# The second layer's value projection moved ahead as seven half-size products, and its head steps cut to three weight chunks

## The chip, the cores and the metric

The kernel runs on one core of a Trainium2 chip. The metric is the device time in microseconds from the first to the last instruction of one execution, taken as the median of several runs. In the profile the engines are PE (TensorE matmul), PEld (its weight loads), DVE (VectorE), ACT (ScalarE), POOL (GpSimd) and SP (SyncE, which here only issues DMAs).

## The reference, cut to what matters

Two transformer blocks run one after the other over 512 tokens with 2048 channels, in float32. The first block is untouched except that work is put beside its last two stages. The second block is

```
h = x1 @ w_in_2                       # 2048 -> 8192 columns
qa, ka, va, ga, qb, kb, vb, gb = split(h)      # 1024 columns each, 16 heads of 64
ya = dilated_attention(qa, ka, va) * silu(ga)        # 16 heads "A"
yb = neighbourhood_attention(qb, kb, vb) * silu(gb)  # 16 heads "B"
out = layer_norm(alpha * x1 + concat(ya, yb) @ w_out_2)
```

`x1` is the first block's output. The change concerns `va` and `vb` (all 2048 value columns) and the order of the work around the two attentions.

## The kernel before, in words

Every float32 matrix product is done as three matmuls on split operands: high part by high part, low by high and high by low (`mm3`, L454 to L458). Weights come as one stream of chunks of 1 MB (128 partitions x 2048 float32). SP loads a chunk into one of two buffers `w_raw`, ACT copies its high part into `w_hi` (`split_hi`, L436 to L440), DVE subtracts to get `w_lo` (`split_lo`, L442 to L445), and PE uses both (`chunk_ready`). The counters `hi_ready`, `lo_ready` and `chunk_used` count chunks; chunk c can be split once chunk c-2 has been used. A chunk of 256 weight columns and 8 tiles of the inner dimension takes 48 matmuls of 512 columns.

The stages that matter, in order of time:

- **Up** (about 1157 to 1325 us): 8 groups of two chunks (`up_group` on PE, `up_out` on DVE). For each group POOL loads 1.5 MB of gates (`load_gates`, L2905) into the single tile `mixg` once DVE has read the last ones; DVE's first use (`gated`, L2406) stands ahead of its `split_lo` of the next group's first chunk.
- **Output projection of block 1** (about 1326 to 1500 us): 8 groups of two chunks (`wo_group` on PE, `x1_out_of` on DVE). It leaves x1 in `act_b`, high and low parts, two of 16 tiles per group. DVE adds the residual (L2445), ACT makes the high part, DVE the low part (L2452).
- **Head-pair steps** (about 1500 to 2286 us): 16 groups of four chunks. Step s multiplies x1 with the columns of query, key, value and gate of one pair of heads (128 columns each): chunks cc 0 and 1 give query and key, cc 2 and 3 give value and gate. In the same step PE does the attention of the pair before it, in two bursts (`beat`): ahead of chunk 0, and ahead of chunk 2. A burst has the logits of two units (`qk2`, L1160) and the products of two earlier units' probabilities with the values (`pv2`, L1181). Steps 1 to 8 attend over A heads (kind "A2"), steps 9 to 16 over B heads ("M2" on PE, "N2" on POOL).
- **Last product** (2286 us to the end): `w_out_2`, then the layer norm.

Between logits and `pv2` a unit goes through a chain: DVE adds the bias and takes the maximum (`soft2_a`, L2472 or L2476), ACT takes the exponential (`exp2`), DVE divides by the sum (`soft2_b`, L2492 and L1806) and transposes 32x32 blocks (`flip2`, L2505 or L2510), POOL stores the result to HBM (`flip_store`, L2989) and loads it back turned (`flip_load`, L3000, into `prob_t`). For A heads units 0 and 1, whose logits are in the first burst, are read by the second burst of the same step, and units 2 and 3 by the first burst of the next step. For B heads every unit is read one whole step later. The values are transposed by DVE (L2589), stored (L2970) and loaded as `v_tok_a` or `v_tok_n` (L2977, L2980) in every step. At each step's end ACT takes a tanh of the gate (L1749) and DVE finishes it (L2593).

All orders are written out by hand, one in-order program per engine, with semaphores between them.

Of the kernel before, what the change touches and what calls it, by code (L numbers as in the profile page):

```python
# [19 lines left out]
F32 = mybir.dt.float32  # L20
# [5 lines left out]
P = 128  # L26
# [20 lines left out]
G_UP, G_WO, G_IN2, G_OUT2 = 52, 60, 68, 100  # L47
N_GROUPS = 108
G_S0, G_S1 = G_Q + 2, G_MIX + 6
C_S0 = 2 * G_S0  # L50
SLOT_KB = (16, 20, 32, 36, 24, 28, 40)

# [83 lines left out]
def build_kernel(nc, wst, xt_in, mem_in, par_in, con_in, pos_in, tab1_in, tab2_in, rpb_in, lng_in, lnb_in, out):  # L136
# [18 lines left out]
    v2_d = nc.dram_tensor("v2_d", [T, P], F32)  # L155
# [6 lines left out]
    with ctx:  # L162
# [86 lines left out]
        th_2 = sb_at("th_2", [P, 2, T], RA + 44 * KB)  # L249

# [98 lines left out]
        par_s, con_s, pos_s = sem("params_loaded"), sem("con_loaded"), sem("pos_loaded")  # L349
# [4 lines left out]
        mem_s = [sem(f"mem_loaded{i}") for i in range(8)]  # L354
        x_s = [sem(f"x_loaded{i}") for i in range(8)]
        mh_s, ml_s = sem("mem_hi"), sem("mem_lo_and_x_sums")
        sq_s, sq_used, rows_s = sem("squares_and_x_sums_hi"), sem("squares_used_and_x_sums_lo"), sem("row_sums_copied_and_quarter_chain")
        stm_s, stx_s = sem("mem_sums_psum"), sem("x_sums_psum")
# [43 lines left out]
        v2_stored, v2_loaded = sem("v2_stored"), sem("v2_loaded")  # L402
# [33 lines left out]
        def split_hi(act, c, s, early=False):  # L436

            act.wait_ge(w_loaded[s], 8 * (c - s) - 16)
            act.wait_ge(chunk_used, c - 3 if early else c - 1)
            act.activation(w_hi[s][:], w_raw[s][:], ACT.Copy).then_inc(hi_ready, 1)  # L440

# [105 lines left out]
        def in2_banks(kind, cc):  # L547

            return (0, 1) if cc < 2 or kind == "A2" else (4, 5) if kind else (6, 7)
# [34 lines left out]
        def _(sp):  # L584
# [46 lines left out]
            with sp.Fori(G_IQ, G_OUT2 + 1) as g:  # L631
                for s in range(2):
                    sp.wait_ge(lo_ready, 2 * g + s - 1)
                    sp.dma_start(w_raw[s][:], wst[2 * g + s]).then_inc(w_loaded[s], 16)

            def last_weights(c):
                sp.wait_ge(lo_ready, c - 1)
                sp.dma_start(w_raw[c % 2][:], wst[c]).then_inc(w_loaded[c % 2], 16)
# [5 lines left out]
            sp.wait_ge(chunk_used, 2 * G_OUT2 - 1)  # L644
# [29 lines left out]
        def _(pe):  # L674
# [512 lines left out]
            pe.wait_ge(x1f_s, 18)  # L1187
            pe.wait_ge(x1h_s, 9)
            pe.wait_ge(x1l_s, 7)
# [20 lines left out]
            def pair_step(step, par, kind, before, gemm=True):  # L1210

                for cc in range(4):
                    if kind and cc % 2 == 0:
                        beat(kind, before, step, cc // 2, par)
                    g = 2 * step + (G_IN2 + cc // 2)
                    if cc % 2 == 0 and before:
                        if kind == "A2" or (before == "A2" and cc == 0):
                            pe.wait_ge(ev_act, evac_act(step, cc // 2 - 1))
                            pe.wait_ge(ev_dve, evac_dve(step, cc // 2 - 1))
                        elif before == "M2":  # L1220
                            pe.wait_ge(ev_act, evac_act(step - 1, cc // 2))
                            pe.wait_ge(ev_dve, evac_dve(step - 1, cc // 2))
                    elif cc == 2 and kind:
                        pe.wait_ge(ev_act, evac_act(step, 0))
                        pe.wait_ge(ev_dve, evac_dve(step, 0))
                    chunk_ready(pe, 2 * g + cc % 2)
                    rows_t(pe, cc % 2, range(6), act_b, in2_banks(kind, cc))
                    if cc == 1 and not kind:
                        pe.wait_ge(x1h_s, 10)
                        pe.wait_ge(x1l_s, 8)  # L1230
                    rows_t(pe, cc % 2, range(6, 8), act_b, in2_banks(kind, cc)).then_inc(chunk_used, 1)
# [8 lines left out]
            with pe.Fori(0, 3) as i:  # L1240
                pair_step(2 * i + 10, 1, "M2", "M2")
                pair_step(2 * i + 11, 0, "M2", "M2")
            def y_split(pe, k):
# [34 lines left out]
            pe.wait_ge(ev_act, evac_act(15, 1))  # L1278
            pe.wait_ge(ev_dve, evac_dve(15, 1))
# [47 lines left out]
        def _(act):  # L1327
# [368 lines left out]
            with act.Fori(0, 4) as i:  # L1696
                for s in range(2):
                    g = 2 * i + (G_WO + s)
                    hi2(g)
                    act.wait_ge(x1f_s, 4 * i + (2 * s + 6))  # L1700
                    copy(act_b[0][:, bass.ds(4 * i + 2 * s, 2), :], stage[s][:]).then_inc(x1h_s, 1)
# [21 lines left out]

            def pair_step(step, par, kind, before, new, final=False):

                for cc in range(4):
                    g = 2 * step + (G_IN2 + cc // 2)
                    if kind:
                        split_hi(act, 2 * g + (cc % 2 + 1), 1 - cc % 2)
                        if cc % 2 == 0:  # L1730
                            for c in (cc, cc + 1):
                                exp2(kind, step, c)
                    if new:
                        if not kind:
                            split_hi(act, 2 * g + (cc % 2 + 1), 1 - cc % 2)
                        if cc == 1:
                            summed(g)
                            dst, src = q_rows(new, qkvg[1 - par][0][:], bank[0][:])
                            copy(dst, src)
                            dst, src = q_rows(new, q_raw[new == "N2"][:], bank[0][:])  # L1740
                            copy(dst, src).then_inc(ev_act, 1)
                        elif cc == 3:
                            if final:
                                for p in range(2):
                                    y_hi(p)
                            summed(g)
                            if not (isinstance(step, int) and step == 0):
                                act.wait_ge(ev_dve, evac_dve(step - 1, 1))
                            act.activation(th_2[:, par, :], bank[in2_banks(kind, cc)[1]][:], ACT.Tanh, scale=0.5).then_inc(ev_act, 1)  # L1749
# [13 lines left out]
            split_hi(act, 2 * G_OUT2 + 1, 1)  # L1763
# [5 lines left out]
            split_hi(act, 2 * G_OUT2 + 2, 0)  # L1769
            split_hi(act, 2 * G_OUT2 + 3, 1)  # L1770
# [3 lines left out]
            def last_split_hi(c):  # L1774

                act.wait_ge(w_loaded[c % 2], 8 * (2 * G_OUT2 + c - c % 2) - 16)
# [3 lines left out]
            def rows_out(n_out):  # L1780
                for c in range(1 if n_out else 3, 5):
# [3 lines left out]
                    if 4 * n_out + c < 13 and (n_out or c > 3):  # L1785
                        split_hi(act, 2 * G_OUT2 + 4 * n_out + c, c % 2)
# [13 lines left out]
        def _(dve):  # L1800
# [636 lines left out]
            def x1_out_of(i, s):  # L2437
# [8 lines left out]
                if not (isinstance(i, int) and i == 3):  # L2446
# [4 lines left out]
                dve.wait_ge(x1h_s, 2 * i + (s + 3))  # L2451
                dve.tensor_tensor(act_b[1][:, bass.ds(4 * i + 2 * s, 2), :], stage[s][:],  # L2452
                                  act_b[0][:, bass.ds(4 * i + 2 * s, 2), :].bitcast(F32), ALU.subtract).then_inc(x1l_s, 1)

# [81 lines left out]
            def beat_dve(kind, before, step, cc, par, split):  # L2536

                if cc % 2 == 0:
                    if cc == 0 and kind == "A2":
                        dve.wait_ge(b2_loaded[par], bias2_count(step, par))  # L2540
                    elif cc == 0:
                        dve.wait_ge(nb_ready, 2 * step - 16)
                    for c in (cc, cc + 1):
                        soft2_a(kind, step, c, par)
                    split()
                    for c in (cc, cc + 1):
                        soft2_b(kind, step, c)
                        if kind == "A2" or c % 2:
                            flip2(kind, step, c)
                else:  # L2550
                    if before == ("A2" if cc == 1 else "M2"):
                        gated2(before, step - 1, 1 - par)
                    split()

            def pair_step(step, par, kind, before, new, final=False):

                for cc in range(4):
                    g = 2 * step + (G_IN2 + cc // 2)
                    split = lambda: split_lo(dve, 2 * g + (cc % 2 + 1), 1 - cc % 2)
                    if kind:  # L2560
                        beat_dve(kind, before, step, cc, par, split)
                    if new:
                        if not kind:
                            split()
                        if cc == 1:
                            summed(g)
                            q_l, k_l = qk_lo(new, 1 - par)
                            q_h, k_h = qkvg[1 - par][0:2]
                            if new == "A2" and isinstance(step, int) and step == 0:
                                for s in range(2):  # L2570
                                    dve.wait_ge(x1_out[s], 416)
                            dve.tensor_scalar(k_h[:], bank[1][:], HD2 ** -0.5, None, ALU.mult).then_inc(x1h_s, 1)
# [558 lines left out]
```

## Time and profile before

| | us |
|---|---|
| median of 3 runs | 2478.37 (2478.15 to 2479.02) |
| span of the profiled execution | 2477.0 |
| PE busy in the profiled execution | 2464.3 (99%) |
| DVE, ACT, POOL busy | 1506.1, 841.0, 696.6 |
| mean granted TensorE clock | 0.999 |
| DMA, mean over the span | 183 GB/s |

A busy time counts an engine's instructions, not its waits. PE's busy time is near the span because its matmuls follow each other; each is listed with some 390 ns though one starts every 227 ns, since they overlap in the array. So distances between start times are read, not durations. The profiled execution's own time is known only as this span, which lies 1.4 us under the median of the runs.

### The profile page before, as it was taken

What the parts mean: (1) busy time and instruction counts of PE and PEld (TensorE: products, weight loads), DVE (VectorE), ACT (ScalarE), POOL (GpSimd) and SP (SyncE); (2) the same over time, 40 slices, a digit from 0 to 9 for tenths busy, and PEclk for the clock granted to TensorE, in tenths of its full rate; (3) what the DMA queues carried; (4) which work ended last, traced back from release to release, by engine and by line L of the source; (5) the groups of instructions that cost most, each with busy time, mean ns of one, the idle gap of its engine ahead of it and who ended that gap; (6) DMA issues with size and microseconds to landing.
All of it is one profiled execution on the core that took longest, in us unless ns stands there. A gap on an engine that the chain in (4) does not pass through costs nothing.

```text
span 2477.0 us, 36169 instructions
## 1 busy us (share of the span) xinstructions
PE 2464.3 (99%) x13712; PEld 2092.3 (84%) x13712; DVE 1506.1 (61%) x2529; ACT 841.0 (34%) x1281; POOL 696.6 (28%) x867
## 2 busy tenths in 40 slices
PE   9999999999999999999999999999999999999998
PEld 7788899999988888888888888888888888888887
DVE  5664877898779976655554333556465545455525
ACT  7422444544454333333222222223232322223221
POOL 0312455666512222232001220211122334343100
PEclk9999999999999999999999999999999999999999
DMA  7748333433456766777544444676656555546622
GB/s 287 223 162 271 114 126 128 130 135 136 137 173 211 259 230 237 241 244 274 178 165 149 136 153 128 205 196 205 205 176 212 172 175 160 171 153 214 242 96 102
DMA packets 102405, 452.53 MB, mean 183 GB/s; under 512 B 18006, under 2 KB 18006, under 8 KB 74182
## 3 DMA queue, kind: packets, MB, share of 16 engines
q1 hardware_dynamic: 38712, 241.58, 28.7%
q0 software_dynamic: 63568, 209.25, 26.8%
q8 instruction: 82, 1.34, 0.2%
q14 instruction: 43, 0.35, 0.0%
HBM read 351.47 MB, written 100.79 MB: 183 GB/s over the span
## 4 chain that ended last, share of the span: by engine, by line
PE 98%; DMA 1%; SPq 0%; DVE 0%; ACT 0%; issue 0%; DVEq 0%
PE bank L456 23%; PE bank L457 22%; PE bank L458 22%; PE bank L874 16%; PE bank L1258 5%; PE bank L1181 2%; PE bank L1319 2%; PE bank L1160 2%; PE bank L1043 1%; PE bank L1018 1%; DMA w_raw<-wst 1%; PE bank L955 1%; PE bank L1038 0%; PE bank L1008 0%; PE bank L898 0%; PE bank L713 0%
## 5 line engine op out<-in xcount | busy, mean ns | idle before, releaser
L445 DVE TENSOR_TENSOR w_lo<-w_raw,w_hi 128x2048 fp32r<-128x2048 f32 x164 | 375.9, 2292 | 369.5 <-ACT w_hi L440 367.3
L456 PE MATMUL bank<-act_b,w_hi 128*128 128x512 f32 x1280 | 501.6, 392 | 0.0
L457 PE MATMUL bank<-act_b,w_lo 128*128 128x512 f32 x1280 | 498.4, 389 | 0.0
L458 PE MATMUL bank<-act_b,w_hi 128*128 128x512 f32 x1280 | 498.1, 389 | 0.0
L440 ACT ACTIVATE w_hi<-w_raw 128x2048 fp32r<-128x2048 f32 x163 | 311.7, 1913 | 509.6 <-PE bank L458 435.9
L456 PE MATMUL bank<-act_a,w_hi 128*128 128x512 f32 (+1 forms) x1032 | 405.8, 393 | 0.0
L457 PE MATMUL bank<-act_a,w_lo 128*128 128x512 f32 (+1 forms) x1032 | 401.9, 389 | 0.0
L458 PE MATMUL bank<-act_a,w_hi 128*128 128x512 f32 (+1 forms) x1032 | 401.8, 389 | 0.0
L456 PEld LDWEIGHTS bank<-act_b,w_hi 128*128 128x128 f32 x1280 | 240.2, 188 | 54.5 <-issue 5.2
L458 PEld LDWEIGHTS bank<-act_b,w_hi 128*128 128x128 f32 x1280 | 240.3, 188 | 50.4
L457 PEld LDWEIGHTS bank<-act_b,w_lo 128*128 128x128 f32 x1280 | 240.3, 188 | 48.8
L874 PE MATMUL bank<-t_xh,pt_w 128*128 128x256 f32 x1280 | 232.1, 283 | 0.0
L456 PEld LDWEIGHTS bank<-act_a,w_hi 128*128 128x128 f32 (+1 forms) x1032 | 193.4, 187 | 42.3 <-issue 1.4
L458 PEld LDWEIGHTS bank<-act_a,w_hi 128*128 128x128 f32 (+1 forms) x1032 | 193.4, 187 | 41.2
L457 PEld LDWEIGHTS bank<-act_a,w_lo 128*128 128x128 f32 (+1 forms) x1032 | 193.5, 188 | 39.1
L874 PEld LDWEIGHTS bank<-t_xh,pt_w 128*128 128x128 f32 x1280 | 199.7, 192 | 0.0
L874 PE MATMUL bank<-act_a,pt_w 128*128 128x256 f32 x1440 | 181.5, 283 | 0.0
L874 PE MATMUL bank<-t_xl,pt_w 128*128 128x256 f32 x640 | 181.1, 283 | 0.0
L2105 DVE TENSOR_TENSOR pt_w<-s_sum,pt_w 128x512 fp32r<-128x512 f32 x160 | 157.9, 1003 | 37.1 <-ACT pt_w L1332 36.3
L874 PEld LDWEIGHTS bank<-act_a,pt_w 128*128 128x128 f32 x1440 | 176.2, 192 | 3.0 <-issue 1.6
L2766 POOL TENSOR_TENSOR s_sum<-w_raw 128x512 f32<-128x512 f32 x80 | 120.7, 1520 | 108.7 <-DMA w_raw<-wst 70.4
L1332 ACT ACTIVATE pt_w<-s_sum 128x512 fp32r<-128x512 f32 x160 | 100.5, 630 | 94.0 <-PE bank L874 82.9
(376 smaller groups left out, 3351.7 us busy)
## 6 DMA issues: line engine op xcount, KB each, us to landing
w_raw<-wst SPq DMA_DIRECT2D x210, 1024.0 KB, 5.0
prob_t<-flip_d POOLq DMA_DIRECT2D x64, 512.0 KB, 4.8
flip_d<-flip POOLq DMA_DIRECT2D x56, 512.0 KB, 4.3
mix_d<-stage POOLq DMA_DIRECT2D x24, 512.0 KB, 3.2
mixg<-mix_d POOLq DMA_DIRECT2D x8, 1536.0 KB, 6.8
prob_tk<-flip_d POOLq DMA_DIRECT2D x32, 256.0 KB, 6.0
flip_d<-flip_a POOLq DMA_DIRECT2D x16, 512.0 KB, 2.9
b<-rows_2d POOLq DMA_DIRECT2D x16, 448.0 KB, 10.3
```

The lines of the kernel that those rows point to most:

```text
L440: act.activation(w_hi[s][:], w_raw[s][:], ACT.Copy).then_inc(hi_ready, 1)
L445: dve.tensor_tensor(w_lo[s][:], w_raw[s][:], w_hi[s][:].bitcast(F32), ALU.subtract).then_inc(lo_ready, 1)
L456: pe.matmul(out_ap, l_hi, r_hi, start=start, stop=False)
L457: pe.matmul(out_ap, l_lo, r_hi, start=False, stop=False)
L458: return pe.matmul(out_ap, l_hi, r_lo, start=False, stop=stop)
L874: last = pe.matmul(quarter(g, i), pt_w[i][l][:, j, :], x_part(c, i, r, j), start=(i % 2 == 0 and c == 0 and j == 0 and m == 0), stop=(c == ...
L1160: ins = pe.matmul(logit_bank(kind, step, cc, e)[:, off:off + w], q[half, c * P:(c + 1) * P], keys(k, half), start=(n == 0), stop=(n == 2))
L1181: last = pe.matmul(bank[O_BANK][64 * e:64 * e + 64, c * P:(c + 1) * P], v[:, b, 64 * e:64 * e + 64], turned[:, e, b], start=(b == 0), stop ...
L1258: last = pe.matmul(bank[4 * s + b][:], act_b[l][:, k, b * P:(b + 1) * P], wt(r[c % 2], kt, 0, 2 * GC, 2 * GC), start=(k == 0 and n == 0), ...
L1332: return act.activation(dst, src, ACT.Copy, **kw)
L2105: dve.tensor_tensor(pt_w[i][1][:], w_part(c, i), pt_w[i][0][:].bitcast(F32), ALU.subtract)\
L2766: pool.tensor_tensor(dst[:], l, r, op).then_inc(ws_s, 1)
```

## The change

Value columns leave the head-pair steps. Before step 0 a new stage computes all values at once. For each of the two layers' halves (n = 0: A heads, n = 1: B heads) the 512 x 2048 by 2048 x 1024 product is cut in halves in all three dimensions and done as seven products of 256 tokens x 1024 x 512 columns (the Winograd form of Strassen's scheme), each of two chunks of 24 matmuls. The tokens are now the stationary operand.

- Weight sums: four per half, each 2 MB, made HBM to HBM by POOL's DMAs during the up stage (`w_sums_2`: four copies, then four accumulating DMAs in three stages, each after the one before).
- Sums of x1: DVE makes four of 128x256 per tile pair in the output projection, POOL stores them and loads them back at the stage's start, ACT and DVE split them.
- Results: ACT and DVE combine the seven products from PSUM (`values_first`, `values_read`), POOL stores 16 tiles to HBM (`values_store`).
- Three raw weight buffers instead of two in this stage.

A step then has three chunks: two for query and key, one for the gate (PSUM bank 7). The second burst stands in the middle of the second chunk for A heads (k = 12 of 16), and between the second and the third chunk for B heads. DVE's transpose of the values and POOL's store of them go; `load_v` loads from the table.

DVE's order in a step of kind "A2" changes too, see below. The load of the attention outputs for the last product (`load_y`) waits for the middle of step 15's gate chunk; it waited for the chunk ahead of the last one.

```diff
@@ SP
+            for n in range(2, PARTS_V):
...
+                sp.dma_start(w_raw_v[slot][:], src).then_inc(wv_loaded[slot], 16)
...
-            sp.wait_ge(chunk_used, 2 * G_OUT2 - 1)
+            sp.wait_ge(half_g, 17)
@@ PE: the new stage
+                for kc in range(2):
+                    c = C_VAL + 2 * p + kc
+                    chunk_ready(pe, c)
+                    for jj in range(4):
+                        j = 4 * kc + jj
...
+                        for b in range(2):
+                            for m, (l, r) in enumerate(((0, w_hi), (1, w_hi), (0, w_lo))):
+                                last = pe.matmul(v_banks(p)[b][:], v_stationary(q, l, j, b), wt(r[c % 2], jj, 0, 512, 512),
+                                                 start=(j == 0 and m == 0), stop=(j == 7 and m == 2))
+                    last.then_inc(chunk_used, 1)
@@ PE: a step
+                if kind:
+                    beat(kind, before, step, 0, par)
...
+                for m in range(2):
...
+                        if kind == "A2" and k == A2_BEAT:
+                            beat(kind, before, step, 1, par)
...
+                if kind == "M2":
+                    beat(kind, before, step, 1, par)
...
+                for k in range(KT):
+                    last = mm3(pe, bank[G_BANK][:], ...)
+                    if last_step and k == CK - 1:
+                        last.then_inc(half_g, 1)
@@ DVE: output projection
+                dve.tensor_tensor(t1, b12, b11, ALU.subtract).then_inc(xs_new_s, 1)
+                dve.tensor_tensor(t3, b22, b12, ALU.subtract).then_inc(xs_new_s, 1)
...
+                dve.tensor_tensor(t2, b22, t1, ALU.subtract).then_inc(xs_new_s, 1)
...
+                dve.tensor_tensor(t4, t2, b21, ALU.subtract).then_inc(xs_new_s, 1)
@@ DVE: a step of kind "A2", m = 1
+                        if m == 1 and before == "A2":
+                            gated2(before, step - 1, 1 - par)
+                        split()
+                        if m == 1:
+                            for c in (2, 3):
+                                soft2_a(kind, step, c, par)
...
+                    if new and m == 1:
+                        dve.wait_ge(chunk_used, in2_chunk(step, 2))
...
+                        dve.tensor_scalar(k_h[:], bank[1][:], HD2 ** -0.5, None, ALU.mult).then_inc(x1h_s, 1)
...
+                        dve.tensor_tensor(q_l[:], q_raw[new == "N2"][:], q_h[:].bitcast(F32), ALU.subtract)\
+                            .then_inc(x1l_s, 1)
+                    if kind == "A2" and m == 1:
+                        for c in (2, 3):
+                            soft2_b(kind, step, c)
                             flip2(kind, step, c)
@@ POOL: up stage
+            def w_sums_2(v, stage_):
+                if v or stage_:
+                    pool.wait_ge(ws_done, 128 * v + (0, 64, 96, 112)[stage_])
+                if stage_ == 0:
+                    for dst, summand in ((2, 0), (0, 2), (1, 3), (3, 1)):
+                        w_sum(v, dst, "w", summand)
+                elif stage_ == 1:
+                    w_sum(v, 2, "w", 2, True)
+                    w_sum(v, 0, "w", 3, True)
...
+            for j in range(1, 8):
                 pool.wait_ge(up_ev, 3 * j + 3)
                 pool.nop(nofuse=True)
                 load_gates(j)
+                w_sums_2((j - 1) // 4, (j - 1) % 4)
```

## Rows read from the trace of the kernel before

**Rows 1.** The page: shares of the chain that ended last, by engine.
```profile
PE 98%; DMA 1%; SPq 0%; DVE 0%; ACT 0%; issue 0%; DVEq 0%
```

**Rows 2.** Waits of PE: who waited for whom, total us, times, longest.
```profile
PE bank L742 <- POOL warm L2682: 1.6, 1, 1.6
```

**Rows 3.** The chain in order of time: start us, length us, what.
```profile
1643.92 1.59 PE bank L1160 x12
1645.52 1.90 PE bank L1181 x32
...
1694.90 1.59 PE bank L1160 x12
...
2045.36 0.93 PE bank L1160 x12
2046.29 1.02 PE bank L1181 x16
...
2286.64 1.59 PE bank L1258 x6
...
2324.28 98.15 PE bank L1258 x432
```

**Rows 4.** Timeline of DVE, second burst of an A step: start, us, instruction, idle before.
```profile
1669.48 0.69 DVE L2572 TENSOR_SCALAR qkvg<-bank 128x512 fp32r<-128x512 f32 x1 [6.64 <-PE bank L458]
...
1676.65 0.16 DVE L2492 RECIPROCAL rden<-rs 128x1 f32<-128x1 f32 x1
```

**Rows 5.** Timeline of POOL in the same step, both bursts.
```profile
1660.88 0.77 POOL L3000 DMA_DIRECT2D prob_t<-flip_d  x1 [1.84 <-DMA flip_d<-flip_a]
...
1685.91 0.77 POOL L3000 DMA_DIRECT2D prob_t<-flip_d  x1 [0.57 <-DMA flip_d<-flip_a]
```

**Rows 6.** The tile prob_t, 30 loads of 1575 to 1945 us: issue to landing.
```profile
DMA to landing us min/median/max: 4.1/4.6/8.3
```

**Rows 7.** Timeline of DVE and ACT around the output projection's end.
```profile
1489.54 1.92 ACT L440 ACTIVATE w_hi<-w_raw 128x2048 fp32r<-128x2048 f32 x1 [6.60 <-PE bank L458]
...
1491.49 2.29 DVE L445 TENSOR_TENSOR w_lo<-w_raw,w_hi 128x2048 fp32r<-128x2048 f32 x1 [6.22 <-ACT w_hi L440]
1500.42 1.29 DVE L2445 TENSOR_TENSOR stage<-bank,xr 128x512 f32<-128x512 f32 x2 [6.64 <-PE bank L458]
1502.95 1.23 DVE L2452 TENSOR_TENSOR act_b<-stage,act_b 128x1024 fp32r<-128x1024 f32 x1 [1.23 <-ACT act_b L1332]
```

**Rows 8.** Timeline of SP, ACT and DVE at the last steps' end.
```profile
2273.84 1.02 SPq L642 DMA_DIRECT2D o_raw<-y_d  x2
...
2280.05 1.92 ACT L1332 ACTIVATE act_b<-o_raw 128x2048 fp32r<-128x2048 f32 x1 [4.23 <-DMA o_raw<-y_d]
...
2286.78 0.58 ACT L1749 ACTIVATE th<-bank 128x512 f32<-128x512 f32 x1
...
2292.01 2.28 DVE L2388 TENSOR_TENSOR act_b<-o_raw,act_b 128x2048 fp32r<-128x2048 f32 x1
```

**Rows 9.** Timeline of DVE and POOL in one group of the up stage.
```profile
1195.85 1.29 DVE L2406 SCALAR_TENSOR_TENSOR m_tmp<-mixg,bank 128x512 f32<-128x512 f32 x2 [4.25 <-PE bank L458]
...
1205.06 1.29 DVE L2406 SCALAR_TENSOR_TENSOR m_acc<-mixg,bank 128x512 f32<-128x512 f32 x2 [1.26 <-DMA mixg<-mix_d]
1208.61 2.29 DVE L445 TENSOR_TENSOR w_lo<-w_raw,w_hi 128x2048 fp32r<-128x2048 f32 x1 [2.26 <-ACT w_hi L440]
...
1197.98 0.77 POOL L2905 DMA_DIRECT2D mixg<-mix_d  x1 [20.80 <-DVE m_tmp L2406]
```

**Rows 10.** DMA of 210 to 250 us, GB/s in 40 slices of 1 us; one issue.
```profile
GB/s 315 381 340 250 410 397 397 414 270 205 131 115 102 111 102 94 102 111 164 193 295 344 393 410 430 397 418 463 422 389 430 414 401 348 348 352 262 94 16 0
...
rows_n<-rpb POOLq DMA_DIRECT2D x1, 1472.0 KB, 14.9
```

**Rows 11.** Timeline of POOL and DVE in a step over B heads.
```profile
2119.20 7.86 POOL L2959 TENSOR_TENSOR nb<-nl,con 128x256 f32<-128x256 f32 x8 [8.82 <-DMA nl<-rows_n]
...
2126.56 1.25 DVE L2510 STREAM_TRANSPOSE flip_n<-prob 128x1024 f32<-128x1024 f32 x1
```

More of the change, by code:

```diff
@@ L440, in split_hi, with split_hi2, raw_slot, raw_loads @@
             act.activation(w_hi[s][:], w_raw[s][:], ACT.Copy).then_inc(hi_ready, 1)
+        def split_hi2(act, c, s):
+            act.wait_ge(w_loaded[s], 8 * (c - s) - (16 + 8 * (PARTS_V - 2)))
+            act.wait_ge(chunk_used, c - 1)
+            act.activation(w_hi[s][:], w_raw[s][:], ACT.Copy).then_inc(hi_ready, 1)
+        def raw_slot(n):
+            return n if n < 2 else 0 if n == 2 else (2, 1, 0)[n % 3]
+        def raw_loads(n):
+            return sum(raw_slot(m) == raw_slot(n) for m in range(2, n + 1))
+        def v_banks(n):
+            return [bank[2 * (n % 4) + b] for b in range(2)]
+        def v_used(n):
+            return C_VAL + 2 * n + 2
+        def in2_chunk(step, m):
+            return 3 * step + (C_IN2 + m)
+        def in2_buf(par, m):
+            return (m + 1 - par) % 2
         def split_lo(dve, c, s):
@@ L630, in _ @@
                 weights(c)
-            with sp.Fori(G_IQ, G_OUT2 + 1) as g:
+            with sp.Fori(G_IQ, G_VAL + 1) as g:
                 for s in range(2):
@@ L1208, in beat @@
                         pv2("M2", step - 1, cc, 1 - par)
[L1210 to L1231, printed above, removed]
@@ L1722, in y_hi @@
                 copy(act_b[0][:, k0:k1, :], o_raw[:, k0:k1, :]).then_inc(oh_s, 1)
-            def pair_step(step, par, kind, before, new, final=False):
[L1726 to L1749, printed above, removed]
@@ new lines, in values_first @@
+            def values_first(n):
+                if n:
+                    act.wait_ge(v2_ready, 8 * n + 16)
+                else:
+                    act.wait_ge(x1f_s, 20)
+                act.wait_ge(chunk_used, v_used(7 * n))
+                for b in range(2):
+                    last = copy(v_sum[b][:], v_banks(7 * n)[b][:])
+                last.then_inc(v_first, 1)
+            for n in range(1, PARTS_V):
+                values_hi(n)
+                if n in (2, 4, 6, 8):
+                    x_sums_hi(n // 2 - 1)
+                if n % 14 == 3:
+                    values_first(n // 14)
@@ new lines, in _ @@
+            split_hi2(act, C_IN2, 0)
+            def pair_step(step, par, kind, before, new, final=False):
+                for m in range(3):
+                    if kind or new:
+                        split_hi2(act, in2_chunk(step, m + 1), in2_buf(par, m + 1))
+                    if kind and m == (0, 1 if kind == "A2" else 2)[m > 0]:
+                        for c in (0, 1) if m == 0 else (2, 3):
+                            exp2(kind, step, c)
+                    if new and m == 1:
+                        act.wait_ge(chunk_used, in2_chunk(step, 2))
+                        dst, src = q_rows(new, qkvg[1 - par][0][:], bank[0][:])
+                        copy(dst, src)
+                        dst, src = q_rows(new, q_raw[new == "N2"][:], bank[0][:])
+                        copy(dst, src).then_inc(ev_act, 1)
+                    elif new and m == 2:
+                        if final:
+                            for p in range(2):
+                                y_hi(p)
+                        act.wait_ge(chunk_used, in2_chunk(step, 3))
+                        if not (isinstance(step, int) and step == 0):
+                            act.wait_ge(ev_dve, evac_dve(step - 1, 1))
+                        act.activation(th_2[:, par, :], bank[G_BANK][:], ACT.Tanh, scale=0.5).then_inc(ev_act, 1)
@@ L2534, in last_lo @@
                     .then_inc(olo_s, 1)
[L2536 to L2548, printed above, removed]
-                            flip2(kind, step, c)
[L2550 to L2553, printed above, removed]
@@ new lines, in values_read @@
+            def values_read(n, q):
+                dve.wait_ge(chunk_used, v_used(7 * n + q))
+                if q == 1:
+                    dve.wait_ge(v_first, n + 2)
+                elif q > 2:
+                    dve.wait_ge(v_read, 3 * n + {3: 2, 4: 3, 5: 3, 6: 4}[q])
+                src = v_banks(7 * n + q)
+                for b in range(2):
+                    if q == 1:
+                        values_out(n, b, 0, src[b][:], v_sum[b][:], ALU.add)
+                    elif q == 2:
+                        last = dve.tensor_tensor(v_sum[b][:], src[b][:], v_sum[b][:], ALU.subtract)
+                    elif q == 3:
+                        last = dve.tensor_tensor(v_rest[b][:], v_sum[b][:], src[b][:], ALU.subtract)
+                    elif q == 4:
+                        values_out(n, b, 1, v_rest[b][:], src[b][:], ALU.subtract)
+                    elif q == 5:
+                        values_out(n, b, 2, src[b][:], v_rest[b][:], ALU.add)
+                        last = dve.tensor_tensor(v_sum[b][:], src[b][:], v_sum[b][:], ALU.add)
+                    else:
+                        values_out(n, b, 3, src[b][:], v_sum[b][:], ALU.subtract)
+                if q in V_SUMS:
+                    last.then_inc(v_read, 1)
```

344 lines of the change are left out of this document (262 added, 82 removed).

## The prediction

> **What bounds the kernel now.** I read the chain that ended last first. 98% of it is PE [rows 1], so a gain must come from fewer matmuls, and any new wait of PE is paid in full. The waits of PE came second: it waits for another engine once to a visible extent, 1.6 us at the start [rows 2]. Third, the chain in order of time, for distances. From one first burst to the next an A step takes 1694.90 - 1643.92 = 50.98 us, of which a burst is 1.59 + 1.90 = 3.49 us, twice; a burst over B heads is 0.93 + 1.02 = 1.95 us. In the last product 432 matmuls take 98.15 us, 0.2272 us each [rows 3]. An A step's 192 matmuls take (50.98 - 6.98) / 192 = 0.229 us each, the same plus a refill behind each burst. So I count 0.227 us per matmul of 512 columns, 10.9 us per chunk of 48. Last I read DVE, ACT and POOL around the two bursts, since that slack is what the change spends.
>
> **The saving.** The steps lose one chunk of 48 matmuls each, 16 x 48 = 768. The new stage has 2 x 7 products x 8 tiles x 2 token blocks x 3 = 672. Both have 512 moving columns, and with tokens stationary the last product runs at 0.2272 us [rows 3]. Net 96 x 0.227 = **-21.8 us**. All else is at best neutral.
>
> **The second burst of an A step.** In the new order DVE takes the maximum for units 2 and 3, then waits for the end of the second chunk, makes the key and query parts, and only then divides, transposes and hands units 2 and 3 to POOL. The next step's first burst needs them. Take the second chunk's end as 0.
> - DVE starts the key part 0.4 us after a chunk's end (the burst's first matmul at 1669.06 by the same timeline, the key part at 1669.48 [rows 4]) and has three instructions of 0.69 us that overlap slightly: divisions begin at 2.5.
> - From the first reciprocal to the issue of the last `prob_t` load is 1685.91 - 1676.65 = 9.26 us [rows 4, 5], and the load lands 4.6 us later in the median, 4.1 to 8.3 [rows 6]. DVE's split stands ahead of that chain before and behind it after, so it is not in these 9.26. The last unit is there at 2.5 + 9.3 + 4.6 = 16.4.
> - PE wants it after the gate chunk, 10.9, then the logits, 1.6, then the product with the other unit, 0.95 (half of 1.90): 13.5 with 0.1 for the switch.
> So PE waits 2.9 us. DVE's split of the next chunk now ends about when the two loads are issued (2.5 + 5.1 of divisions and transposes + 2.3 = 9.9), and frees a raw buffer: a 1 MB weight load starts beside them. At the 410 GB/s of full slices [rows 10] 1 MB is 2.6 us; I give the last load 0.6 us of it. That makes 3.5 us per step, in steps 2 to 9 (the first burst of each reads A units of the step before): 8 x 3.5 = **+28 us**. Bounds: 2.4 us with the shortest landing and no contention, 19 in all; 5 us if a load takes 6.5 us, 40 in all. Before, the same units had 1676.65 - 1669.06 = 7.6, + 9.3 + 4.6 = 21.5 us against 21.8 + 3.5 + 2.6 = 27.9, so 6 us of slack; one chunk less with the key part kept ahead of them uses more than that.
>
> Units 0 and 1 have less trouble. Their last load is issued 1660.88 - 1643.92 = 17.0 us after the burst's start [rows 3, 5] and lands at 21.6; PE wants it at 3.5 + 10.9 + 5.5 + 1.6 + 0.95 = 22.4, later still by the 3.5 us that PE has just waited. I cost it at nothing; without that cover it is 0 to 1 us.
>
> **Steps over B heads.** A step shrinks to 144 x 0.227 + 3.9 = 36.6 us. Units are read a step later, so the DMA round trip has room. DVE is the fuller engine: its transpose ends at 2126.56 + 1.25, 10.6 us behind the key part's start (2117.20 by the same view) [rows 11]; after it comes the 0.85 us of the output gate, all before the gate chunk ends (10.9 + 1.95 = 12.9). POOL's 7.86 us of window bias begins 9 to 10 us after its loads' issue and ends near 32 of 36.6 us. Nothing; if one of them is late, some 1 us x 8.
>
> **The new stage.** A chunk of 24 matmuls takes 5.45 us. Splitting one takes 1.92 on ACT and 2.29 on DVE; ACT starts at the earlier chunk's end and DVE ended at 1493.78, 4.2 us after ACT's start at 1489.54 [rows 7], some 4.6 after the chunk's end. It fits with 0.8 us left. Reading a product adds two PSUM operations of 0.65 (four after the sixth), 1.3 or 2.6 us of DVE per two chunks: 4.6 + 2.6 = 7.2, while the next split can begin at 5.45 + 2.3 = 7.8. Nothing in the likeliest case; 0.5 us in each of 27 chunks, 13 us, if waits between them add up.
> Its start is late. DVE begins the last x1 tiles at 1500.42 and ends their low part at 1504.18 [rows 7]. Then come the four new sums of 128x256 (about 0.4 each, under the 0.65 of 512 columns, with two hand-overs: 1.8) and the split of the second chunk, 2.3: 1508.3. PE ends the first chunk at 1500.1 + 5.45 = 1505.6: **+2.7 us**. Its end is smooth but for one weight load that must land in 6.2 us: +0.3.
>
> **The end.** The loads for the last product are issued 5.4 us ahead of step 15's end instead of 10.9. The first was split by ACT 6.2 us after issue [rows 8], so at +0.8, +2.7 done, +5.0 with DVE's 2.3. PE comes to it 2.0 us after the end (2286.64 - 2284.6 [rows 3]): some 3 us of wait. The second load delays ACT's tanh and all of DVE's later work by 3 to 6 us, and DVE's low part before ended at 2294.3, just ahead of PE [rows 8]; both shift together. **+3 us**, bounds 1 and 6.
>
> **The up stage.** POOL queues 8.4 MB of copies and later 4.2, 2.1 and 2.1 MB of accumulating DMAs behind one gate load and ahead of the next. Now DVE's first gate use starts 7.1 us after the issue and is followed by the split at 1208.61, which PE needs at 1195.4 + 21.8 = 1217.2 [rows 9]. So a gate load may be some 8 us late. Copies and weights of a group, 8.4 + 2.1 MB, at 410 GB/s take 25.6 us, 4 to 5 us past the next gate load's issue. That hides. The only HBM to HBM transfer of the trace, `rows_n`, ran in slices of 390 to 460 GB/s in all [rows 10]. No row shows an accumulating DMA. Bounds: as a copy, 10 us for 4.2 MB, and at the 102 GB/s of the slowest busy slices [rows 10], 41 us. I take half the copy's rate, 20 us, hidden. At the far end each 4.2 MB makes gates 11 us later than 30 us allows, twice; with copies at half rate too, four times: 22 to 44 us.
>
> The Trainium skill, "DMA: Bandwidth & Descriptors", section on latency and other measured facts, gives 207 to 214 GB/s per direction for copies between HBM tensors. Rows 10 show nearly twice that for one small copy, so they disagree so far. By the page 8.4 MB take 39 us, and the skill's "Collectives: The Full Stack", section on the bandwidth ceiling, has an add need two source reads, at half a copy's rate; by both the up stage would come near the 44 us above, which is the far end of the late gates below.
>
> **Sum.** -21.8 + 28 + 2.7 + 0.3 + 3 = **+12.2 us**. On the span 2477.0 that is 2489.2; the median of the runs is 1.4 us above the span, so 2490.6.
>
> **Rivals.**
> - *The wait isn't there (faster).* If DVE's chain or the round trip is 3 us shorter than in the rows, or PE has other work there, only -21.8 + 6 = -16 remains: 2462. For it: POOL has less to do, no store of values competes, and 13.5 against 16.4 is a narrow miss. Against it: 9.26 us is the common distance, and the wait for the second chunk is in the order itself. It decides at 2.0 us per step; below that the change is faster. At 2.0 to 3.2 us it is within the measurement.
> - *The gates come late too (slower still).* Place: the up stage, groups 2, 3, 6 and 7. It decides if accumulating DMAs move under 140 GB/s. Price 22 to 44 us: 2513 to 2535.
> - *The value stage falls behind.* Its margin is 0.8 us per chunk. 13 us more: 2504. For it: DVE, ACT and 3 load buffers all turn in 5.45 us; against it: each part's durations fit.
> - *The clock falls at the waits.* The granted clock was 0.999 over the whole run, so at most 2.5 us in all were lost to the level of 1.2 GHz. If every one of 8 waits cost that once more, 20 us: 2511. The waits are short and split in two by a product, which speaks against it. The Trainium skill, "TensorE: Matmul & The Clock Gate", "What's actually happening", says idleness brings the lower level back; no wait in this trace tests it.
>
> **Chances.** Forecast 0.52, no wait 0.22, late gates 0.13, value stage 0.09, clock 0.04. The likeliest's own range is 2481 to 2500. The range for all, 2465 to 2513, leaves out half of the late gates and the best of the faster case. No change is what lies within 0.2%, 5 us, all that a measurement can tell. Faster is the 0.22 and 0.04 of the forecast's low tail: 0.26. Within 0.2% I put 0.15, the forecast with 2.0 to 3.2 us per wait. Slower: 0.59.
>
> **What would show it.** Right: L1181's first burst of steps 2 to 9 starts late, PE idle 3 to 4 us released by the DMA into `prob_t`, an A step of 43 to 44 us and a B step near 37; a new stage of 153 us with one wait of 2 to 3 us at its second chunk for `w_lo`; a wait of 3 us after step 15. Wrong: A steps of 40 us, PE waits under `mixg` in the up stage, value chunks further apart than 5.5 us, or a granted clock under 0.99.

## The result, and the profile after

| | median | runs | profiled run: span, mean granted clock |
|---|---|---|---|
| before | 2478.26 us | 4: 2477.57 to 2479.02 | 2477.0 us, 0.999 |
| after | 2547.35 us | 4: 2542.33 to 2553.53 | 2546.0 us, 0.985 |

The ratio is 1.0279, interval 1.0264 to 1.0295: slower by 69 us. The sign was forecast, but the time lies 57 us above the forecast and 34 us above the range's end.

The chain that ended last was PE to 98% [rows 1]. The same line of the page now says:

```profile
PE 85%; DMA 8%; DVE 3%; issue 2%; SPq 1%; ACT 0%; POOL 0%; DVEq 0%; POOLq 0%; ACTq 0%
```

PE waited visibly once [rows 2]. Its waits now (released line, releaser, total us, times, longest):

```profile
PE bank L1250 <- DMA prob_t<-flip_d: 32.0, 12, 4.7
PE bank L505 <- DVE w_lo L494: 15.2, 3, 5.7
PE bank L505 <- DVE m_tmp L2556: 6.1, 1, 6.1
PE bank L1380 <- DVE act_b L2538: 2.7, 1, 2.7
PE bank L1292 <- DVE w_lo L2704: 2.2, 1, 2.2
PE bank L811 <- POOL warm L2898: 1.6, 1, 1.6
```

Three of them were in the forecast: L1250 (28 us there), L1380 (3) and L1292 (2.7). The two at L505 lie in the up stage, which was costed at nothing. The waits sum to 58 us more than before; less the 21.8 us forecast as saved that makes 36 of the 69. The rest, some 33 us, has to be slower work between the waits, and the granted clock shows it. By stretch (length, busy us of each engine with instructions, PEclk, DMA share, GB/s):

```profile
1180.00:1260.00 80.00, 69.25 (x287) 56.38 (x287) 35.91 (x33) 14.35 (x10) 6.01 (x8) 0.91 1.01 315
1300.00:1360.00 60.00, 49.50 (x201) 40.04 (x200) 25.82 (x25) 9.66 (x6) 4.34 (x5) 0.90 0.99 286
1360.00:1530.00 170.00, 170.00 (x749) 140.67 (x748) 73.08 (x73) 38.28 (x24) 43.86 (x65) 1.00 0.58 183
1760.00:2100.00 340.00, 308.41 (x1700) 248.18 (x1699) 185.27 (x388) 97.43 (x164) 67.01 (x103) 0.94 0.60 193
2100.00:2280.00 180.00, 180.00 (x969) 146.62 (x968) 97.71 (x252) 56.05 (x109) 69.57 (x96) 1.00 0.53 166
```

In the three of these stretches where PE waits, the clock is low too. The first two rows are the up stage, with all DMA engines full; the fourth is the steps over A heads. In the kernel before PE was busy in all of these and the clock 1.00.

What one wait costs is seen in the chain of one A step (start, length, what):

```profile
1896.76 8.17 DMA prob_t<-flip_d
1904.97 3.68 PE bank L1250 x32
1908.66 0.73 PE bank L505
1909.38 0.43 PE bank L506
1909.81 0.43 PE bank L507
1910.23 0.43 PE bank L505
1910.66 0.37 PE bank L506
1911.03 0.23 PE bank L507
```

PE waited 4.7 us for this load. The product (32 small matmuls) then takes 3.68 us where it took 1.90 [rows 3], and matmuls stand 0.43 us apart (the level of 1.2 GHz) for another 2.4 us before they are 0.23 apart again (2.4 GHz).

The up stage by the same view:

```profile
1184.27 25.85 DMA w_raw<-wst
1210.14 1.92 ACT w_hi L465
1212.08 2.30 DVE w_lo L494
1214.52 0.76 PE bank L505
...
1229.22 20.86 DMA mixg<-mix_d
...
1250.89 0.68 DVE m_acc L2556
1251.57 2.21 DVE w_lo L494
1254.01 0.79 PE bank L505
```

A weight load of 1 MB takes 25.85 us, and the gate load 20.86 (6.7 to 7.0 before). First the split is late for want of weights, then because DVE's gate use, ahead of it in DVE's order, waits for the gates. PE waited four times in this stage: until 1214.5 us (5.7) and 1315.4 (4.4), both for weights loaded beside four queued copies, and until 1254.0 (5.0) and 1356.7 (6.1), both behind a gate load that stood beside accumulating transfers. What the DMA engines were given, by POOL's issues: four copies at 1178.8 and again at 1281.1, then each time two accumulating transfers together (1213.3, 1313.9), then two more one by one (1246.6 and 1261.4, 1348.2 and 1363.4). Some of them:

```profile
L3140 POOL DMA_DIRECT2D wsum_d<-wst x4: 493/493/547, 1281.1 to 1282.6; - x4
DMA to landing us min/median/max: 11.8/21.5/31.0
...
L3138 POOL DMA_DIRECT2D wsum_d<-wst x2: 947/1107/1267, 1213.3 to 1213.9; - x2
DMA to landing us min/median/max: 19.8/26.1/32.4
...
L3138 POOL DMA_DIRECT2D wsum_d<-wsum_d x1: 907/907/907, 1246.6 to 1246.6; - x1
DMA to landing us min/median/max: 14.5/14.5/14.5
```

**Where the 69 us are.** In the chain the long piece of the value stage begins at 1540.92; a chunk of 5.45 and the wait of 2.2 lie ahead of it, so the output projection ends at 1533.3 instead of 1500.1: +33. By the same reckoning it ends at 1529.3 in experiment 1 and 1530.3 in experiment 5 below, whose work is the same up to there; so some 4 us of the 33 vary from one execution to the next. The second bursts of the steps over A heads start at 1786.89, 1832.30, 1878.68, ..., 2064.45, 46.3 us apart, where 40.1 is what such a step takes without the wait (in an experiment below): 8 x 6.2 = +50. With -22 for the matmuls that leaves +8 for start, end and what the clock adds there.

### The profile page after: what moved, and what is told of

Read it like the earlier page. It is cut to its first block, busy times and chain, and to the rows that moved or that the text cites. A ratio compares the mean times of both kernels' runs of the same rounds, so it can differ in the third digit from the quotient of the medians.

```text
span 2546.0 us, 36092 instructions
## 1 busy us (share of the span) xinstructions
PE 2474.0 (97%) x13616; PEld 2094.6 (82%) x13616; DVE 1552.1 (61%) x2589; ACT 874.1 (34%) x1301; POOL 706.3 (28%) x894
## 4 chain that ended last, share of the span: by engine, by line
PE 85%; DMA 8%; DVE 3%; issue 2%; SPq 1%; ACT 0%; POOL 0%; DVEq 0%; POOLq 0%; ACTq 0%
PE bank L505 17%; PE bank L506 16%; PE bank L507 16%; PE bank L943 16%; PE bank L1292 6%; PE bank L1380 5%; DMA mixg<-mix_d 2%; DMA prob_t<-flip_d 2%; PE bank L1250 2%; PE bank L1439 2%; DMA w_raw<-wst 1%; PE bank L1229 1%; DMA flip_d<-flip 1%; DMA raw_m<-wst 1%; PE bank L1112 1%
## 5 line engine op out<-in xcount | busy, mean ns | idle before, releaser
L494 DVE TENSOR_TENSOR w_lo<-w_raw,w_hi 128x2048 fp32r<-128x2048 f32 x149 | 341.6, 2293 | 348.0 <-ACT w_hi L471 187.9
L505 PE MATMUL bank<-act_b,w_hi 128*128 128x512 f32 x1024 | 407.9, 398 | 15.2 <-DVE w_lo L494 15.2
L505 PE MATMUL bank<-act_a,w_hi 128*128 128x512 f32 (+1 forms) x1032 | 407.0, 394 | 6.1 <-DVE m_tmp L2556 6.1
L506 PE MATMUL bank<-act_b,w_lo 128*128 128x512 f32 x1024 | 403.3, 394 | 0.0
L507 PE MATMUL bank<-act_b,w_hi 128*128 128x512 f32 x1024 | 402.0, 393 | 0.0
L505 PEld LDWEIGHTS bank<-act_b,w_hi 128*128 128x128 f32 x1024 | 195.2, 191 | 62.6 <-issue 22.5
L505 PEld LDWEIGHTS bank<-act_a,w_hi 128*128 128x128 f32 (+1 forms) x1032 | 194.0, 188 | 48.9 <-DVE m_tmp L2556 6.5
L465 ACT ACTIVATE w_hi<-w_raw 128x2048 fp32r<-128x2048 f32 x87 | 166.3, 1911 | 186.7 <-PE bank L507 165.9
L507 PEld LDWEIGHTS bank<-act_b,w_hi 128*128 128x128 f32 x1024 | 195.2, 191 | 41.5
L506 PEld LDWEIGHTS bank<-act_b,w_lo 128*128 128x128 f32 x1024 | 195.5, 191 | 39.6
L471 ACT ACTIVATE w_hi<-w_raw 128x2048 fp32r<-128x2048 f32 x61 | 116.8, 1914 | 267.7 <-PE bank L507 188.5
L2255 DVE TENSOR_TENSOR pt_w<-s_sum,pt_w 128x512 fp32r<-128x512 f32 x160 | 151.3, 958 | 38.1 <-ACT pt_w L1452 37.8
```

The source lines that it names most:

```text
L494: dve.tensor_tensor(w_lo[s][:], w_raw[s][:], w_hi[s][:].bitcast(F32), ALU.subtract).then_inc(lo_ready, 1)
L505: pe.matmul(out_ap, l_hi, r_hi, start=start, stop=False)
L506: pe.matmul(out_ap, l_lo, r_hi, start=False, stop=False)
L507: return pe.matmul(out_ap, l_hi, r_lo, start=False, stop=stop)
L2255: dve.tensor_tensor(pt_w[i][1][:], w_part(c, i), pt_w[i][0][:].bitcast(F32), ALU.subtract)\
```

## Experiments

The kernel before, measured beside them, had a median of 2478.0 us with the first four experiments and 2478.6 with the last three. The ratios are against it.

**1. DVE's order in an A step put back (e1_units_first).**

```diff
 for c in (2, 3):
     soft2_a(kind, step, c, par)
+for c in (2, 3):
+    soft2_b(kind, step, c)
+    flip2(kind, step, c)
```

The same four calls are taken out behind the key part.

> The changed kernel with one part of DVE's order put back: in a step over A heads, division, transpose and hand-over of units 2 and 3 stand ahead of DVE's wait for the second chunk and of the key part. Nothing else is changed. Theory (a chain too long by its place in DVE's order): the last prob_t load is issued 2.5 + 0.4 us earlier or more, so the 32 us of PE's waits at L1250 for the DMA into prob_t fall under 5 us, and with them the low clock between 1760 and 2100 us (0.94 there): an A step falls from 46.3 to 40 to 41 us and the run by 8 x 5.5 = 44 us, to about 2503. Rival (the round trip itself is too slow, or the key part is late next): the waits stay, at half or more of 32 us, or come back behind the key part, and the time stays over 2525.

Measured 2499.84 us, ratio 1.0091 (1.0074 to 1.0108): 47.5 us off the kernel changed, where 44 were expected. The waits:

```profile
PE bank L505 <- DVE w_lo L494: 13.9, 3, 4.8
PE bank L505 <- DVE m_tmp L2556: 6.3, 1, 6.3
PE bank L1250 <- DMA prob_t<-flip_d: 4.1, 5, 1.7
```

L1250 fell from 32.0 to 4.1, the clock of the stage rose to 1.00, and the products at L1250 stand 20.05 us apart, 40.1 per step. The wait was DVE's order, not a round trip that can't be shortened; and nothing else was late right behind. In the profiled executions 4 of the 49 us between the two spans lie ahead of the steps, in the up stage, which the edit doesn't touch; the steps gave some 45.

**2. One weight sum at a time (e2_sums_spread).**

```diff
-w_sums_2((j - 1) // 4, (j - 1) % 4)   # 4 copies, then 2, 1, 1 accumulating
+next_w_sum(j - 1)                     # one transfer, waits for the last one
 ...
 x_sums_store(i, s)
+next_w_sum(8 + 2 * i + s)
```

> The changed kernel with POOL's weight sums spread: the same eight 2 MB transfers per value set, but one at a time, one behind each gate load; the first eight in the up stage as before, the second eight in the output projection's groups. In the kernel changed, four 2 MB copies are queued at once. Theory (the gate and weight loads are starved by several 2 MB transfers that share the DMA engines with them): the waits for w_lo L494 (15.2 us) and m_tmp L2556 (6.1 us) go, a load of mixg takes under 10 us instead of 20 to 21, the granted clock between 1180 and 1360 us returns from 0.9 to 1.0, the output projection ends near 1501 instead of 1533, and the run falls by 25 to 33 us, to 2514 to 2522. Rival (an accumulating DMA of 2 MB costs the up stage as much wherever it lies): waits of 10 us or more remain, in the up stage or moved to the output projection, and the time is over 2535.

Measured 2541.20 us, ratio 1.0258 (1.0241 to 1.0276): only 6 us gained, where 25 to 33 were expected. The up stage came out as the theory had it, and the loss moved on, which was the rival's sign:

```profile
1180.00:1215.00 35.00, 35.00 (x156) 29.01 (x155) 20.54 (x19) 7.48 (x5) 1.77 (x2) 1.00 0.82 274
1215.00:1260.00 45.00, 45.00 (x201) 37.26 (x200) 24.06 (x22) 9.57 (x6) 3.03 (x4) 1.00 0.83 268
...
1300.00:1360.00 60.00, 60.00 (x266) 49.45 (x264) 28.68 (x28) 12.44 (x8) 6.11 (x9) 1.00 0.69 223
1360.00:1420.00 60.00, 53.51 (x228) 43.83 (x228) 22.21 (x22) 11.36 (x7) 18.98 (x29) 0.94 0.82 258
1420.00:1530.00 110.00, 99.18 (x420) 81.14 (x420) 40.73 (x45) 21.75 (x14) 27.23 (x40) 0.94 0.80 239
```

The up stage is clean, PE full and the clock 1.00. In the output projection PE now waits at w_lo L494 for 17.3 us in four waits. The chain there:

```profile
1382.67 0.61 POOL wsum_d L3138
1383.28 19.43 DMA xr<-x_t
1402.89 0.45 issue
1403.34 0.69 DVE stage L2595
```

An x load is issued by POOL right behind a weight sum and lands after 19.43 us (4.0 to 5.7 before); DVE's residual sum waits 15.7 us for it, and the weights' low part stands behind it. All eight x loads of this run are issued behind an accumulating transfer and take 18.6 to 20.0 us, while the gate loads of the up stage, issued just ahead of a transfer, take 6.7 to 7.2. So what counts is what stands ahead in the same queue; an x load behind a copy was not tried.

**3. Both (e3_both).** The edits of 1 and 2 in one kernel.

> Both edits at once: units 2 and 3 ahead of DVE's wait, and the weight sums one at a time over two stages. If the two losses are independent, the gains add up: 44 + 30 = 74 us, about 2473, which is 5 us under the kernel before; what is left of the saving of 21.8 us is then eaten by the starts and ends (2.7 + 2.2 + 1.6 us of waits and their refill) and by the low clock after them. Rival (a step with less slack has another wait right behind: DVE's or ACT's chain): 2485 to 2500 and PE waits for DVE or ACT in the A steps.

Measured 2496.08 us, ratio 1.0077 (1.0060 to 1.0094). 45.1 us below experiment 2, as 1 stood 47.5 below the kernel changed: the two losses are independent. The expected 2473 was missed by 23 us all the same, since it counted 30 us for the second edit, which gave 6 in experiment 2 and 4 here. The time lies in the rival's range, but its reason doesn't hold: PE's waits in the A steps are 3.9 us in all, and for prob_t. By the same reckoning as above the output projection ends at 1524.3, so 24 us of the second loss are left.

**4. The weight sums alone, in the kernel before (e4_before_with_sums).** The kernel before with the sixteen transfers of the change, in its schedule.

> The kernel before with POOL's sixteen weight-sum transfers of 2 MB added to its up stage in the schedule of the kernel changed; they read other rows of the weights, of the same size, and nobody reads their result. No matmul, no order of DVE and no step is changed. Theory (the loss of the up stage is these transfers alone, not DVE's order nor anything behind): PE waits of 15 us for w_lo and 6 us for m_tmp appear, the granted clock between 1180 and 1360 us falls to 0.9, the output projection ends 33 us later than 1500, and the time is 2478 + 33 = 2511. Rival (the x sums and DVE's changed order in the output projection are half of the loss): under 2497.

Measured 2507.08 us, ratio 1.0118 (1.0101 to 1.0135): +29 us, with PE, DVE and the steps as before; the rival would have had it under 2497.

```profile
PE bank L458 <- DVE w_lo L447: 13.8, 3, 5.1
PE bank L458 <- DVE m_tmp L2408: 6.4, 1, 6.4
```

The clock of 1180 to 1215 is 0.91 and of 1300 to 1360 0.91. DVE begins the last residual sums at 1527.95 instead of 1500.42, 27.5 us later, against 29 to 33 in the three runs of the changed up stage. So the transfers make the loss; the rest is 2 to 6 us, about what those runs differ by among themselves. Copies and accumulating transfers were not added separately.

**5. The wait filled with work (e5_filled_wait).**

```diff
 elif before == "A2" and pair == 0:
+    for n in range(14):
+        pe.matmul(bank[0][:], act_b[0][:, 0, 0:P], act_b[0][:, 0, :], start=True, stop=True)
     for cc in range(2, 4):
         pv2("A2", step - 1, cc, 1 - par)
```

> The changed kernel with 14 extra matmuls of 512 columns (14 x 0.227 = 3.2 us at full clock) in the first burst of each step over A heads that follows another, ahead of the product that waits for prob_t; their result is overwritten, nothing else is changed. In the kernel changed an A step takes 46.3 us where the matmuls and the wait of 4 us make 44.0, and the granted clock of 1760 to 2100 us is 0.94. Theory (idle time of PE, not the late load as such, brings the clock down, 2.3 us per step beyond the wait): the extra work fills the wait, the granted clock of that stage rises to 0.99 or more, a step falls to 44 us although PE does more, and the run by 16 to 18 us against the kernel changed (2547), to about 2530. Rival (the 2.3 us are something else, slower matmuls beside the loads or refills): the step stays at 46 us or grows by what is not covered, and the time is 2545 to 2560.

Measured 2531.23 us, ratio 1.0209 (1.0192 to 1.0226): 16.1 us faster than the kernel changed, with more work for PE.

```profile
1760.00:2100.00 340.00, 331.81 (x1866) 265.66 (x1866) 185.52 (x383) 97.05 (x164) 73.79 (x110) 1.00 0.61 196
```

The clock of the stage is 1.00 instead of 0.94, a step 44.6 us instead of 46.3. What is left of PE's wait at L1250 is 8.5 us, the longest 1.3, and the clock doesn't fall at waits of that length here. The step of 46.3 is 40.1 + 4.0 of wait + 2.2; the one of 44.6 is 40.1 + 3.2 of extra matmuls + 1.1 of wait + 0.3. So the lower clock cost 1.9 to 2.2 us a step, 15 to 17 in all, and of the 50 us of the A steps 32 are the wait. That the whole run gained 16.1 as well is partly chance: 13 of them lie in these steps and 3 ahead of them, in the part that varies.

**6. The sums where the DMA engines have room (e6_sums_early).** Experiment 1's order; the first value set's eight transfers one by one in the query and gate projections, the second's in the up stage.

```diff
 for g in range(G_S0, G_S1):
     ...
+    if 0 <= g - G_S0 - 1 < 8:
+        next_w_sum(g - G_S0 - 1)
 ...
-next_w_sum(j - 1)
+next_w_sum(j + 7)
```

> Units 2 and 3 ahead of DVE's wait, as in e1_units_first, and the weight sums again one transfer at a time, but those of the first value set in eight groups of the query and gate projections (300 to 560 us, where the DMA engines are busy 39% of the time) and those of the second one behind the gate loads of the up stage; none is left in the output projection but the last. Theory (e3_both lost 24 us to the x loads of the output projection, which stood behind a weight sum in the same queue, 19.3 us where they need 5): the output projection ends at 1500 to 1502, no wait for w_lo L494 over 1 us, and the run is 24 us under e3_both, at 2472, 6 us faster than the kernel before. Rival (the transfers delay the weight loads or POOL's quarter sums of the projections as well): the time is over 2480, and a wait or a late end shows before 700 us.

Measured 2474.69 us (10 runs, 2469.97 to 2477.41), ratio 0.9984 (0.9974 to 0.9994). 21.4 us under experiment 3, where 24 were expected, and 4 us under the kernel before, where 6 were: ahead of it by its interval, by less than the 0.2% that count as a difference here.

```profile
300.00:560.00 260.00, 258.49 (x2146) 253.27 (x2146) 233.42 (x273) 125.37 (x204) 167.96 (x120) 1.00 0.62 194
...
1180.00:1260.00 80.00, 80.00 (x354) 66.28 (x353) 46.68 (x42) 19.15 (x12) 6.06 (x8) 1.00 0.82 269
```

The price of the early transfers is 1.5 us of PE. The output projection ends at 1504.0, 4 us late (1500 to 1502 were expected). This run also lets the saving be read. From the output projection's end to PE's first matmul of the last product the kernel before takes 2286.6 - 1500.1 = 786.5 us, this one 2275.7 - 1504.0 = 771.7, with 5.9 us of waits in it (2.2, 2.8 and 0.9): without them it would be 20.7 us shorter than before, where the count of matmuls gave 21.8.

**7. Start and end (e7_start_and_end).** Experiment 6, and:

```diff
 for n in range(2):
+    sp.wait_ge(half_g, 17 + n)        # after k tile 4, after k tile 8
     load_y(n)
 ...
+dve.wait_ge(hi_ready, C_VAL + 2)      # last x1 tile, ahead of the x sums
+dve.tensor_tensor(w_lo[1][:], w_raw_v[1][:], w_hi[1][:].bitcast(F32), ALU.subtract).then_inc(lo_ready, 1)
```

> e6_sums_early, and two edits: DVE splits the second chunk of the value stage ahead of the four x sums of the last tile, and the first load for the last product is issued after the fourth and the second after the eighth k tile of step 15's gate chunk, where both waited for the eighth. Theory (both waits are late hand-overs, and nothing else is late right behind): the waits at L1292 (2.2 us) and L1380 (2.8 us) fall to under 0.5 and to about 1, and with the low clock after each the run is 4 to 6 us under e6_sums_early, at 2467. Rival (the next hand-over is as late: the x sums in the value stage, the second load or DVE's low parts at the end): under 2 us gained, and the wait appears at another line.

Measured 2474.16 us (10 runs, 2471.20 to 2485.05), ratio 0.9985 (0.9974 to 0.9996): nothing gained, where 4 to 6 us were expected. PE's waits:

```profile
PE bank L1251 <- DMA prob_t<-flip_d: 6.1, 5, 2.5
...
PE bank L1293 <- DVE w_lo L2708: 1.9, 1, 1.9
...
PE bank L1293 <- DVE w_lo L2615: 1.5, 1, 1.5
...
PE bank L1381 <- DVE act_b L2539: 0.2, 1, 0.2
```

Both waits moved on instead of going, as the rival had it. At the end act_b is there almost in time (0.2 us instead of 2.8), but 9 us later a product waits 2.5 us for prob_t; at the start the second chunk waits 1.5 and the third 1.9, where the second alone waited 2.2. The other waits for prob_t lie in the A steps and are 3.5 us in all, where experiment 6 had 0.9; no run says why.

## Why the prediction was wrong, and where it was right

- **The saving, -21.8 us**: held; 20.7 by experiment 6. In the kernel changed a B step is 2165.10 - 2128.11 = 36.99 us by the chain (36.6 forecast), an A step without waits 40.1 (experiment 1), and the value stage's long piece is 148.7 us for 648 matmuls, 0.2295 each (0.2272 forecast, 1.5 us in all).
- **The second burst, +28 us**: right in mechanism and place, and near in size. 32.0 us were measured, 4.7 the longest, and experiment 1 takes it away with DVE's order alone. Loads into prob_t of 1575 to 1945 us took 5.8 us in the median (4.6 before [rows 6], 4.4 in experiment 1); the forecast gave the last one 5.2. It also let PE do one unit's product, 0.95 us, ahead of the wait. In five of the eight steps it was the first of the two loads that ended the wait, 6.8 to 8.2 us after its issue, and both products ran behind it in one piece (the 32 matmuls at 1904.97 above).
- **The clock at those waits, chance 0.04**: wrong. The rival's own price, 20 us, was close to the 16 of experiment 5. What spoke against it ("the waits are short and split in two by a product") had no row behind it: the trace of before held no wait of this length after its start. It should have been part of the forecast, or a large chance. The up stage's waits had the same follow-up, 0.90 and 0.91 in its two rows.
- **The up stage, "I take half the copy's rate, 20 us, hidden"**: the step that failed. The term was 0 and its far end 44; 33 us came (29 to 33 in three runs). Three values under it were wrong. One is the copy's rate: 410 GB/s were the slices of a stretch with many transfers [rows 10], and `rows_n` by itself, 1.5 MB in 14.9 us, was the row of a transfer. A copy of 2.1 MB takes 10.0 us in the median with moderate traffic (experiment 6, 300 to 600 us), 210 GB/s. Four of them queued at 1178.8 kept the engines full until 1213.3, 34.5 us for 8.4 MB, 243 GB/s. The Trainium skill's "DMA: Bandwidth & Descriptors", section on latency and other measured facts, gives 207 to 214 GB/s for copies between HBM tensors on the queues of SP and ACT. The single copy here, issued by POOL, agrees with it, and the four together are above it. I let a row that showed something else outweigh it. The second is the accumulating transfer, for which no row stood: two of them, 4.2 MB, issued at 1213.3, took until 1246.6, 33 us (126 GB/s) where I took 20. The third is the sharing. I asked when the copies end against the *next gate load*. But a weight load is issued every 10.9 us on SP's queue, and beside four copies one took 25.85 us. The slack itself was well read: a gate load may take 7.1 + 8 = 15 us by the forecast; those of 1229.2 and 1331.6 took 20.9 and 20.2, and PE waited 5.0 and 6.1 us.
- **The reason behind the rival of late gates** (accumulating transfers under 140 GB/s): its price of 22 to 44 us was right, and so was half of its account. The two queued together moved at 126 GB/s, and singly, with moderate traffic, one takes 15.6 us, 134 GB/s. Two of the four waits of PE, 11.1 us, came through gates that were late beside them. The other two, 10.1 us, came through weights that were late beside the copies, which it didn't have. The gate load of 1258.1, beside accumulating transfers one at a time, took 8.8 us, and PE stayed full from 1260 to 1300 us.
- **The value stage** kept up, as forecast: 0.2295 us per matmul over 27 chunks. Start 2.2 (2.7 forecast), end 2.7 (3).
- **No wait, faster**: fell with 32.0 us at L1250.

The forecast with the two rivals in it, 12.2 + 33 + 16 = +61, leaves 8 of the 69: 4 from the longer A waits, 1.5 from the slower matmuls of the value stage, and some 2 that I can't assign. What stays open as well: whether it was the bytes that waited or the number of transfers in the queue that starved the loads, since experiment 2 changed both; and how the loss divides between copies and accumulating transfers, beyond the four waits above. And the runs of experiments 6 and 7 spread over 7 and 14 us where those of before spread over 2; no run separates the cause.

## What to carry to other kernels

When PE is the chain, put two prices on a new wait: its length, and the slower matmuls behind it; here a wait of 4 us cost 6. Background transfers between HBM tensors have to be rated by a row of such a transfer, and against every load that shares the engines, the shortest deadline first (here weights each 10.9 us, x loads behind a sum in the same queue), not against the one that follows in the same program. Before a chunk is taken out of a loop, look at which chains were sized by the chunk's length: the order that keeps the chain into the next product ahead of a wait was worth some 45 us here.

## What the runs showed of the hardware

- A 2.1 MB copy from HBM to HBM lands after 10.0 us in the median (9.7 to 10.8), an accumulating one after 15.6 (15.5 to 17.0), with DMA engines at a share of 0.62 in all; at 0.8 (experiment 6, up stage) it is 11.9 and 18.8. So a single accumulating transfer costs 1.6 times a copy. Queued together in the kernel changed, two accumulating ones moved at 126 GB/s and four copies at 243.
- With four copies queued in POOL's queue, a 1 MB load in SP's queue took 25.85 us; with one, the weights were never late in the up stage. A 0.5 MB load in POOL's own queue right behind an accumulating transfer took 19.4 us (experiment 2) instead of 5.1.
- The wait of 4.7 us that was read closely was followed by 6 us at the 1.2 GHz level; with waits of up to 1.3 us (experiment 5) the stage's granted clock stayed at 1.00.
